# Ending each stage of a three-block transformer token block by token block, and beginning three feed-forward networks token-major

## The chip, the cores and the metric

The kernel runs on one core of a Trainium2 chip (trn2). The time is device microseconds (us) of one execution. TensorE is called PE below, VectorE DVE, ScalarE ACT, GpSimd POOL, and SyncE SP, whose queue issues the loads of the weights.

## The reference

Batch 1, 256 tokens, width 1024, float32. Three blocks run one after the other:

```
def _swiglu(t, w_gate, w_up, w_down):
    return (jax.nn.silu(t @ w_gate) * (t @ w_up)) @ w_down

# block 1, two layers
f = _swiglu(_rmsnorm(h, ffn1_pre_g[l]), ...); h = h + 0.5 * _rmsnorm(f, ffn1_post_g[l])
... attention, three branches ...
h = h + _rmsnorm(merged @ w_out[l], mix_post_g[l])
f = _swiglu(_rmsnorm(h, ffn2_pre_g[l]), ...); h = h + 0.5 * _rmsnorm(f, ffn2_post_g[l])

# block 2, two layers: mixer 0 is a spatial gating unit (SGU), mixer 1 an RWKV scan
x = layer_norm(DN_ALPHA * x + 0.5 * swiglu(x, ffn_w_in[i, 0], ffn_w_out[i, 0]), ...)
x = layer_norm(DN_ALPHA * x + mix, ...)
x = layer_norm(DN_ALPHA * x + 0.5 * swiglu(x, ffn_w_in[i, 1], ffn_w_out[i, 1]), ...)
```

Each feed-forward network (FFN) of blocks 1 and 2 has a hidden width of 2816, there are eight of them. Block 3 is not touched by the change.

## The kernel before

**Tokens.** The 256 tokens are two token blocks of 128 (b = 0, 1; `NB` = 2). The residual stream `h` lies token-major (tokens on partitions). A product needs its input feature-major (`k.x`: features on partitions, 8 tiles of 128 by 256 tokens), so between two stages `h` is normed on DVE and ACT, turned by PE transposes (line 728, `pe_features`), and copied out of PSUM as a rounded part and a rest: `x_hi` on ACT, `x_lo` on DVE (line 750).

**Weights.** All weights come as 440 units of 128x2048 floats (1 MB). SP loads unit n into one of three places of `weight_ring`; `hi` (ACT, line 118) writes the rounded weights and `lo` (DVE, line 313) the rest into one of two slots, `k.w[:, n % 2]`. `hi(n)` waits for the mark of unit n-2, which is the last product that read this slot; PE waits for `lo(n)` before it uses unit n; SP waits for `lo(n-3)` before it loads unit n. Every product is three matmuls (`mm3`, line 105): hi by hi, hi by lo, lo by hi.

**An FFN.** The hidden width is cut in 11 parts of 256. `make(j)` is the gate unit and the up unit of part j (96 matmuls of 256 columns), hidden units on partitions; ACT takes the silu (line 883), DVE multiplies (line 907), ACT and DVE split the hidden values (lines 118 and 910). `use(j)` is the down unit (24 matmuls of 512 columns, 12 for each token block), which adds into four PSUM banks `acc`, two for each token block. The order is make(0), make(1), use(0), make(2), ..., make(10), use(9), use(10). Each engine has one queue, in the order in which the code is written. `act_ffn` and `dve_ffn` put one `hi` and one `lo` behind each part, and one more behind the last: it belongs to a unit of the stage that follows.

**Between the stages.** After a stage, `add(b)` reads `acc` of token block b when that block's last product has been made, so block 0 comes half a unit ahead of block 1. In block 2 (`dve_residual`, `act_residual`) DVE's order is add(0), gain(0), add(1), norm(0), gain(1), norm(1); a block's norm needs the sum of squares and square root from ACT (lines 669, 672). Then follow `pe_features`, which opens with 12 or 24 warm matmuls on constants, and `act_features`. In block 1 (`dve_add_norm`, `act_add_norm`) ACT also reads `acc` itself, once plain and once scaled (lines 606, 613), and a second norm (lines 647 to 659) stands before the turn.

**Names.** ffn1(0), ffn2(0), ffn1(1), ffn2(1) are the FFNs of block 1 (layer in brackets); `f2(0,0)`, `f2(0,2)`, `f2(1,0)`, `f2(1,2)` those of block 2; `sgu` the SGU's down product (8 units), `w_out` the attention's output product (4 units), `w_o` that of the scan (4 units). After `w_o` every engine is drained and waits for all others (`all_drained`, line 335 is its wait).

Of the kernel before, what the change touches and what calls it, by code (L numbers as in the profile page):

```python
# [12 lines left out]
P = 128  # L13
# [210 lines left out]

class Kernel:


    def __init__(self, nc, ctx, aps):
        self.nc, self.ctx, self.aps = nc, ctx, aps
        self.s = Signals(nc, ctx)  # L230
        self.plan, self.unit_marks = [], []
        self.begin()
        self.allocate()

    def begin(self):
# [44 lines left out]
def unit(k, pe, *what, a=KT):  # L280
# [15 lines left out]
def hi(k, act):  # L296
# [3 lines left out]
    if n < len(k.plan):  # L300
        act.wait_ge(*k.s.at(f"w_raw{n % RING}", n))
        if n >= 2:
            act.wait_ge(*k.s.at(*k.unit_marks[n - 2]))
        copy_act(act, k.w.hi[:, n % 2, :], k.ring[:, n % RING, :]).then_inc(*k.s.up("w_hi", n))


def lo(k, dve):
# [368 lines left out]
def dve_residual(k, dve, of, alpha, scale, done):  # L676
# [26 lines left out]
    gain(0)  # L703
    add(1)
    norm(0)
    gain(1)
    norm(1)

# [5 lines left out]
def pe_features(k, pe, of, src, taken, warm=0, at=2, made=None, midway=None):  # L714
# [39 lines left out]
def pe_to_tokens(k, pe, src, ap, start, marks=None):  # L754

    for b in range(NB):
        for c in range(2):
            for i in range(2):
                a = mm3(pe, half(acc_of(k, b), i), src[:, c, b * P:(b + 1) * P], half(ap[:, c], i), start and c == 0)
# [4 lines left out]

def pe_output(k, pe, of, units, ready):

    for n, what in enumerate(units):
# [13 lines left out]
        else:  # L781
            for b in range(NB):
                for j in range(KT):
                    a = tile(b, j)
                if n == 3:
                    a.then_inc(*k.s.up("acc", of, b))
            if n < 3:
                a.then_inc(*k.s.up("out_unit", of, n))
        unit_done(k, *(("acc", of, 1) if n == 3 else ("out_unit", of, n)))
# [41 lines left out]
def pe_ffn(k, pe, f, gate, up, down, ready, beside={}):  # L831

    def make(j):
# [8 lines left out]
        unit_done(k, "gate", f, j, 1)  # L842
        ap = unit(k, pe, *up(j))
        for c in range(2):
# [4 lines left out]
    def use(j):  # L849
        ap = unit(k, pe, *down(j), a=2)  # L850
# [5 lines left out]
        if j < FF - 1:  # L856
            pe_to_tokens(k, pe, k.hid[:, j % 2], ap, j == 0).then_inc(*k.s.up("down", f, j))
            unit_done(k, "down", f, j)
        else:
            pe_to_tokens(k, pe, k.hid[:, j % 2], ap, False, [("acc", f, b) for b in range(NB)])  # L860
            unit_done(k, "acc", f, 1)

    for j in range(FF):
        make(j)
        if j:
            use(j - 1)
        if j in beside:
            beside[j]()
    use(FF - 1)
# [6 lines left out]
def act_ffn(k, act, f, beside={}):  # L876
    def make(j):
# [6 lines left out]
        hi(k, act)  # L884
# [6 lines left out]
    for j in range(FF):  # L891
        make(j)
        if j:
# [3 lines left out]
    hi(k, act)  # L897


def dve_ffn(k, dve, f, beside={}):  # L900
    def make(j):
        lo(k, dve)
        lo(k, dve)
# [9 lines left out]
    for j in range(FF):  # L913
        make(j)
        if j:
# [3 lines left out]
    lo(k, dve)  # L919

def memory1(k, m):
# [3045 lines left out]
```

## Time and profile before

| | |
|---|---|
| Runs shown | 3055.65, 3062.40, 3061.32 us; median 3061.32 |
| Profiled execution, its own time | 3062.81 us |
| Its span in the trace | 3061.0 us |
| Mean granted TensorE clock | 0.975 of full |
| PE busy | 2906.7 us, 95% of the span |
| DVE / ACT / POOL busy | 1704.8 / 1430.4 / 165.4 us |
| Loaded from HBM | 488.32 MB, 160 GB/s |
| A weight unit's load, issue to landing | 4.8 us median |

A start in a row is counted in us from the span's start. "PEclk" is the granted clock. A busy PE is not always one that works on weights: warm matmuls and transposes count too.

### The profile page before, as it was taken

Reading aid. Unit: us, or ns where it says so; the run is one execution under the profiler, and the core shown is the slowest. Engines: PE = TensorE matmul, PEld = TensorE weight load, DVE = VectorE, ACT = ScalarE, POOL = GpSimd, SP = SyncE. Lnnn points to the kernel's source line nnn. Section 1 sums busy time; section 2 is a strip of 40 time slices with the busy share of each in tenths; the row PEclk is TensorE's granted clock in tenths of the full one; section 3 lists DMA queues with packets and bytes.
Section 4 is the critical chain, followed back from the end, with each engine's and each line's share of the span. In section 5 each row is a group of like instructions: output and inputs, shape, how many; then the busy total and the mean of one; then the engine's idle time right before and its main releaser. Section 6 shows DMA issues by size and latency. Waiting matters only on the chain.

```text
span 3061.0 us, 53742 instructions
## 1 busy us (share of the span) xinstructions
PE 2906.7 (95%) x23664; PEld 2700.3 (88%) x23664; DVE 1704.8 (56%) x1977; ACT 1430.4 (47%) x1817; POOL 165.4 (5%) x197
## 2 busy tenths in 40 slices
PE   8999898999998998999999999999987999999998
PEld 8988898999998898999989899899877889876887
DVE  5564555545554556455455654554767454575555
ACT  4455655444455655444445344444551244454444
POOL 1000100000000010001000000000002000054000
PEclk9999999999999999999999999999979999997999
DMA  6553334554553344556554445455420145551453
GB/s 248 189 181 134 138 133 159 192 187 173 192 179 125 137 152 152 191 181 223 191 204 168 153 178 191 171 189 184 151 107 3 48 177 187 179 181 43 152 185 132
DMA packets 69393, 492.87 MB, mean 161 GB/s; under 512 B 7853, under 2 KB 9421, under 8 KB 10534
## 3 DMA queue, kind: packets, MB, share of 16 engines
q1 hardware_dynamic: 64224, 465.53, 42.5%
q10 hardware_dynamic: 4938, 23.92, 2.1%
q8 instruction: 187, 3.06, 0.4%
q14 instruction: 44, 0.36, 0.0%
HBM read 488.32 MB, written 1.06 MB: 160 GB/s over the span
## 4 chain that ended last, share of the span: by engine, by line
PE 80%; DVE 8%; ACT 7%; POOL 2%; issue 2%; PEld 0%; DMA 0%; ACTq 0%; PEldq 0%; DVEq 0%; POOLq 0%; SPq 0%
PE front L105 52%; PE acc L105 28%; ACT weights_hi L118 3%; DVE weights_lo L313 2%; POOL conv_gate L3193 1%; POOL conv_out L3196 1%; DVE tmp L690 1%; DVE h L683 1%; DVE h L698 1%; PEld acc L105 0%; ACT L1111 0%; ACT tmp L1111 0%; DVE b_x_lo L522 0%; ACT b_att_w_by_query L1013 0%; DVE b_x_lo L750 0%
## 5 line engine op out<-in xcount | busy, mean ns | idle before, releaser
L313 DVE TENSOR_TENSOR weights_lo<-weight_ring,weights_hi 128x2048 fp32r<-128x2048 f32 x440 | 1010.0, 2296 | 916.8 <-ACT weights_hi L118 916.5
L105 PE MATMUL front<-b_x_hi,weights_hi 128*128 128x256 f32 x3568 | 1011.0, 283 | 15.5 <-DVE b_x_lo L750 9.9
L118 ACT ACTIVATE weights_hi<-weight_ring 128x2048 fp32r<-128x2048 f32 x440 | 839.7, 1909 | 388.7 <-PE acc L105 355.1
L105 PE MATMUL front<-b_x_hi,weights_lo 128*128 128x256 f32 x3568 | 1005.4, 282 | 0.0
L105 PE MATMUL front<-b_x_lo,weights_hi 128*128 128x256 f32 x3568 | 1004.9, 282 | 0.0
L105 PEld LDWEIGHTS front<-b_x_hi,weights_hi 128*128 128x128 f32 x3568 | 675.3, 189 | 28.9 <-issue 13.3
L105 PEld LDWEIGHTS front<-b_x_lo,weights_hi 128*128 128x128 f32 x3568 | 675.8, 189 | 3.3
L105 PEld LDWEIGHTS front<-b_x_hi,weights_lo 128*128 128x128 f32 x3568 | 674.9, 189 | 0.0
L105 PE MATMUL acc<-weights_hi,b_hidden_hi 128*128 128x512 f32 x832 | 329.6, 396 | 0.0
L105 PE MATMUL acc<-weights_hi,b_hidden_lo 128*128 128x512 f32 x832 | 328.2, 394 | 0.0
L105 PE MATMUL acc<-weights_lo,b_hidden_hi 128*128 128x512 f32 x832 | 327.3, 393 | 0.0
L118 ACT ACTIVATE b_hidden_hi<-act_gate 128x256 fp32r<-128x256 f32 x208 | 86.9, 418 | 341.4 <-DVE act_gate L907 313.4
L883 ACT ACTIVATE act_gate<-front 128x256 f32<-128x256 f32 x176 | 67.3, 384 | 277.5 <-PE front L105 277.4
L105 PEld LDWEIGHTS acc<-weights_hi,b_hidden_lo 128*128 128x128 f32 x832 | 156.5, 188 | 37.8
L105 PEld LDWEIGHTS acc<-weights_lo,b_hidden_hi 128*128 128x128 f32 x832 | 156.7, 188 | 32.7
L105 PEld LDWEIGHTS acc<-weights_hi,b_hidden_hi 128*128 128x128 f32 x832 | 156.5, 188 | 32.6 <-DVE weights_lo L313 0.4
L105 PE MATMUL front<-weights_hi,b_x_hi 128*128 128x256 f32 (+1 forms) x496 | 142.0, 286 | 9.6 <-DVE weights_lo L313 7.6
L105 PE MATMUL acc<-b_x_hi,weights_hi 128*128 128x256 f32 x416 | 124.7, 300 | 20.5 <-ACT tmp L1111 12.7
L105 PE MATMUL front<-weights_lo,b_x_hi 128*128 128x256 f32 (+1 forms) x496 | 141.3, 285 | 0.0
L105 PE MATMUL front<-weights_hi,b_x_lo 128*128 128x256 f32 (+1 forms) x496 | 141.1, 285 | 0.0
L910 DVE TENSOR_TENSOR b_hidden_lo<-act_gate,b_hidden_hi 128x256 fp32r<-128x256 f32 x176 | 75.3, 428 | 85.2 <-ACT b_hidden_hi L118 85.2
L105 PE MATMUL acc<-b_x_hi,weights_lo 128*128 128x256 f32 x416 | 121.0, 291 | 0.0
(493 smaller groups left out, 3904.1 us busy)
## 6 DMA issues: line engine op xcount, KB each, us to landing
weight_ring<-in_weights SPq DMA_DIRECT2D x440, 1024.0 KB, 4.8
xn<-in_norm_rows ACTq DMA_DIRECT2D x14, 1024.0 KB, 4.8
sgu_bias_row<-in_sgu_rows ACTq DMA_DIRECT2D x1, 2048.0 KB, 10.9
sgu_norm_rows<-in_sgu_rows ACTq DMA_DIRECT2D x1, 2048.0 KB, 9.9
bias_hankel<-bias_scratch ACTq DMA_DIRECT2D x1, 1536.0 KB, 6.5
h<-in_x SPq DMA_DIRECT2D x2, 512.0 KB, 6.6
mem_norm<-in_memory SPq DMA_DIRECT2D x1, 1024.0 KB, 14.1
sgu_w_spatial<-in_sgu_w_spatial ACTq DMA_DIRECT2D x1, 1024.0 KB, 4.7
```

The lines of the kernel that those rows point to most:

```text
L105: return pe.matmul(out, a, b, start=start, stop=stop, skip_group_check=True)
L118: return act.activation(out, in_, ACT.Copy, scale=scale)
L313: dve.tensor_tensor(k.w.lo[:, n % 2, :], k.ring[:, n % RING, :], k.w.hi[:, n % 2, :], ALU.subtract) \
L683: dve.scalar_tensor_tensor(out=h, in0=h, scalar=alpha / scale, in1=acc_of(k, b), op0=ALU.mult, op1=ALU.add, accum_out=stat(k, 0, b)).then_ ...
L690: dve.scalar_tensor_tensor(out=k.t[:, b], in0=k.h[:, b, :], scalar=stat(k, 1, b), in1=k.rows[:, 0], op0=ALU.add, op1=ALU.mult).then_inc(*k ...
L698: dve.scalar_tensor_tensor(out=half(k.h[:, b], i), in0=half(k.t[:, b], i), scalar=stat(k, 6, b), in1=half(k.rows[:, 1], i), op0=ALU.mult, ...
L883: act.activation(k.act_gate[:, c, :], k.bank[c][:, 0:S], ACT.Silu).then_inc(*k.s.up("silu", f, j, c))
L910: dve.tensor_tensor(k.hid.lo[:, j % 2, c, :], k.act_gate[:, c, :], k.hid.hi[:, j % 2, c, :], ALU.subtract) \
L3193: pool.tensor_scalar(k.conv_sg[:, 1, :], k.conv_in[:, 1, j:j + S], k.col(("conv_dw_w_3", (0, j)), 1), None, ALU.mult).then_inc(*k.s.up("po ...
L3196: pool.tensor_tensor(k.conv[:, 1, :], k.conv[:, 1, :], k.conv_sg[:, 1, :], ALU.add) \
```

## The change

1. **Last two units block by block.** In `pe_last_two` and in `pe_output` the last two units n-1 and n of a stage run as: unit n-1 for token block 0, unit n for block 0, unit n-1 for block 1, unit n for block 1. This holds for the eight FFNs, the SGU's down product, both `w_out` and `w_o`.
2. **Two more slots.** In the FFNs (of block 2 from the up unit of f2(0,0) on), the SGU's down product and `w_out` a unit takes the one of four slots that has been unused longest; `hi` waits for the unit that used that slot last. Two slots as before hold for the other stages, the attention and `w_o` among them. At two places the second oldest slot is taken (`turned_at`).
3. **hi and lo earlier.** Part 10 of an FFN (`make(10)`) has two `hi` in front of the hidden split and three `lo` in front of the multiplication, and none stands behind the FFN. The SGU's turn has one `hi` and one `lo` ahead of its first `x_hi` and `x_lo`.
4. **Norm order.** `dve_residual` runs add(0), gain(0), norm(0), add(1), gain(1), norm(1).
5. **Token-major head.** The three FFNs behind the norms r2(0,1) (after the SGU, f2(0,2)), r2(0,2) (f2(1,0)) and r2(1,1) (after `w_o`, f2(1,2)) begin with `pe_ffn_head`: turn block 0, gate(0) of block 0, half of up(0) of block 0, turn block 1, the rest of up(0), gate(0) and up(0) of block 1. Here tokens are on partitions, so the hidden values of part 0 are turned back by four more transposes. The 24 warm matmuls of these three places are gone, and the loads of norm rows (`act_load_rows`) are issued behind part 1.
6. **No barrier.** The drain and the waits for all engines behind `w_o` are gone.

```diff
 def hi(k, act):
-        if n >= 2:
-            act.wait_ge(*k.s.at(*k.unit_marks[n - 2]))
-        copy_act(act, k.w.hi[:, n % 2, :], k.ring[:, n % RING, :]).then_inc(*k.s.up("w_hi", n))
+        slot, before = k.place[n]
+        if before is not None:
+            act.wait_ge(*k.s.at(*k.unit_marks[before]))
+        copy_act(act, k.slot[slot].hi, k.ring[:, n % RING, :]).then_inc(*k.s.up("w_hi", n))
...
     add(0)
     gain(0)
+    norm(0)
     add(1)
-    norm(0)
+    if head:
+        dve_x_block(k, dve, of, 0)
     gain(1)
     norm(1)
+    if head:
+        dve_x_block(k, dve, of, 1)
...
+def pe_last_two(k, pe, of, srcs, whats, first_mark, ready):
+    aps = []
+    for b in range(NB):
+        for n in range(2):
+            if b == 0:
+                aps.append(unit(k, pe, *whats[n], a=2))
+                for m in ready[n]:
+                    pe.wait_ge(*k.s.at(*m))
+            a = pe_block_to_tokens(k, pe, srcs[n], aps[n], b)
+            if n:
+                a.then_inc(*k.s.up("acc", of, b))
+            elif b:
+                a.then_inc(*k.s.up(*first_mark))
...
+def pe_ffn_head(k, pe, f, gate, up, of, src, warm):
+    pe_warm(k, pe, warm, 0)
+    pe_turn_block(k, pe, of, src, 0)
+    g, u = unit(k, pe, *gate), unit(k, pe, *up)
+    first, rest = range(KT // 2), range(KT // 2, KT)
+    for b in range(NB):
+        outs = [empty(k, pe, HEAD_BANKS[b][n], (("silu", "glu")[n], f, 0, b))[:, 0:S] for n in range(2)]
+        pe_block_tok(k, pe, of, g, b, outs[0], range(KT)).then_inc(*k.s.up("gate", f, 0, b))
+        if b:
+            unit_done(k, "gate", f, 0, 1)
+            pe_turn_hidden(k, pe, f, 0)
+        pe_block_tok(k, pe, of, u, b, outs[1], first)
+        if b == 0:
+            pe_turn_block(k, pe, of, src, 1)
+        pe_block_tok(k, pe, of, u, b, outs[1], rest).then_inc(*k.s.up("upper", f, 0, b))
+    unit_done(k, "upper", f, 0, 1)
...
 def act_ffn: make(j)
-        hi(k, act)
+        act_units(k, act, 2 if j == FF - 1 else 1)
 def dve_ffn: make(j)
-        lo(k, dve)
-        lo(k, dve)
+        dve_units(k, dve, 3 if j == FF - 1 else 2)
...
 def act_sgu: first turn
+                act.wait_ge(*k.s.at("bias_stored"))
+                hi(k, act)
...
 def pe_rwkv_out, act_rwkv_out, dve_rwkv_out, pool_rwkv_out
-    all_drained(k, pe, "pe", "rwkv")
```

**DVE at the end of f2(0,2)** (part 10 and the norm's first addition; line 907/1100 is the multiplication, 910/1103 the hidden rest, 683/704 add(0)), before:

```order
L313 TENSOR_TENSOR weights_lo<-weight_ring,weights_hi 128x2048 [waits s_w_hi] x3
L907 TENSOR_TENSOR act_gate<-front,act_gate 128x256 [waits s_silu,s_upper]
L910 TENSOR_TENSOR b2_hidden_lo<-act_gate,b2_hidden_hi 128x256 [waits s_hid_hi]
L907 TENSOR_TENSOR act_gate<-front,act_gate 128x256 [waits s_silu,s_upper]
L910 TENSOR_TENSOR b2_hidden_lo<-act_gate,b2_hidden_hi 128x256 [waits s_hid_hi]
L313 TENSOR_TENSOR weights_lo<-weight_ring,weights_hi 128x2048 [waits s_w_hi] x2
L683 SCALAR_TENSOR_TENSOR h,norm_stats<-h,acc 128x1024 [waits s_acc,s_loaded_rows]
```

and now:

```order
L332 TENSOR_TENSOR weights_block20_lo<-weight_ring,weights_block20_hi 128x2048 [waits s_w_hi] x2
L332 TENSOR_TENSOR weights_lo<-weight_ring,weights_hi 128x2048 [waits s_w_hi] x2
L1100 TENSOR_TENSOR act_gate<-front,act_gate 128x256 [waits s_silu,s_upper]
L1103 TENSOR_TENSOR b2_hidden_lo<-act_gate,b2_hidden_hi 128x256 [waits s_hid_hi]
L1100 TENSOR_TENSOR act_gate<-front,act_gate 128x256 [waits s_silu,s_upper]
L1103 TENSOR_TENSOR b2_hidden_lo<-act_gate,b2_hidden_hi 128x256 [waits s_hid_hi]
L332 TENSOR_TENSOR weights_block20_lo<-weight_ring,weights_block20_hi 128x2048 [waits s_w_hi]
L704 SCALAR_TENSOR_TENSOR h,norm_stats<-h,acc 128x1024 [waits s_acc,s_loaded_rows]
```

One `lo` has moved from behind the hidden split to ahead of it: four stand there instead of three, and one instead of two between it and add(0).

**ACT at the end of ffn2(1)**, the last FFN of block 1, part 10 (line 883/1014 is the silu, `s_upper` the mark of part 10's up product, 602/621 the start of the norm), before:

```order
L883 ACTIVATE act_gate<-front 128x256 [waits s_hid_lo,s_gate] x2
L118 ACTIVATE weights_hi<-weight_ring 128x2048 [waits s_gate,s_w_raw0]
L118 ACTIVATE b1_hidden_hi<-act_gate 128x256 [waits s_down,s_glu] x2
L118 ACTIVATE weights_hi<-weight_ring 128x2048 [waits s_upper,s_w_raw1]
L118 ACTIVATE weights_hi<-weight_ring 128x2048 [waits s_down,s_w_raw2]
L602 ACT_TABLE_LOAD
```

and now:

```order
L1014 ACTIVATE act_gate<-front 128x256 [waits s_hid_lo,s_gate] x2
L118 ACTIVATE weights_block10_hi<-weight_ring 128x2048 [waits s_down,s_w_raw1]
L118 ACTIVATE weights_hi<-weight_ring 128x2048 [waits s_upper,s_w_raw2]
L118 ACTIVATE b1_hidden_hi<-act_gate 128x256 [waits s_down,s_glu] x2
L621 ACT_TABLE_LOAD
L625 ACTIVATE act_gate,norm_stats<-acc 128x512 [waits s_acc]
```

Only here does the second `hi` ahead of the hidden split wait for `s_upper`, the last product of part 10 itself; the hidden split that the last down product needs stands behind it.

**DVE between the SGU and f2(0,2)** (683/704 add, 690/711 gain, 698/719 norm, 750/1045 `x_lo`), before:

```order
L313 TENSOR_TENSOR weights_lo<-weight_ring,weights_hi 128x2048 [waits s_w_hi] x2
L683 SCALAR_TENSOR_TENSOR h,norm_stats<-h,acc 128x1024 [waits s_acc,s_loaded_rows]
...
L690 SCALAR_TENSOR_TENSOR tmp<-h,norm_stats,xn 128x1024 [waits s_neg_mean]
L683 SCALAR_TENSOR_TENSOR h,norm_stats<-h,acc 128x1024 [waits s_acc]
...
L698 SCALAR_TENSOR_TENSOR h<-tmp,norm_stats,xn 128x512 [waits s_rstd]
...
L750 TENSOR_TENSOR b2_x_lo<-front,b2_x_hi 128x512 [waits s_x_hi] x2
```

and now:

```order
L704 SCALAR_TENSOR_TENSOR h,norm_stats<-h,acc 128x1024 [waits s_acc,s_loaded_rows]
...
L719 SCALAR_TENSOR_TENSOR h<-tmp,norm_stats,xn 128x512 [waits s_rstd]
L719 SCALAR_TENSOR_TENSOR h<-tmp,norm_stats,xn 128x512
L704 SCALAR_TENSOR_TENSOR h,norm_stats<-h,acc 128x1024 [waits s_acc]
...
L1045 TENSOR_TENSOR b2_x_lo<-front,b2_x_hi 128x4x128 [waits s_x_hi,s_neg_mean]
L1045 TENSOR_TENSOR b2_x_lo<-front,b2_x_hi 128x4x128 [waits s_x_hi]
L711 SCALAR_TENSOR_TENSOR tmp<-h,norm_stats,xn 128x1024
```

Block 0's norm now stands ahead of add(1), and block 0's two `x_lo` between add(1) and gain(1).

## Rows read from the trace of the kernel before

**Rows 1.** The page: span and busy times of the engines.

```profile
span 3061.0 us, 53742 instructions
PE 2906.7 (95%) x23664; PEld 2700.3 (88%) x23664; DVE 1704.8 (56%) x1977; ACT 1430.4 (47%) x1817; POOL 165.4 (5%) x197
```

**Rows 2.** PE's work on constants alone (warm, turns): window, length, busy (count), clock, DMA.

```profile
508.60:518.00 9.40, 7.25 (x63) 1.00 0.24 98
703.90:713.57 9.67, 7.35 (x64) 1.00 0.26 105
1400.00:1406.46 6.46, 5.12 (x40) 1.00 0.90 330
1595.00:1603.70 8.70, 5.41 (x22) 0.73 0.62 262
1759.50:1767.91 8.41, 5.77 (x40) 0.91 0.29 117
1955.60:1964.06 8.46, 5.31 (x40) 1.00 0.30 120
2152.40:2164.72 12.32, 6.22 (x40) 0.76 0.22 86
2454.20:2463.90 9.70, 5.54 (x40) 1.00 0.22 95
2650.80:2659.96 9.16, 6.22 (x40) 0.85 0.26 107
```

**Rows 3.** Chain that ended last, from f2(0,2)'s down(9) to f2(1,0): start, us, what.

```profile
1944.47 5.59 PE acc L105 x24
...
1950.14 1.93 ACT weights_hi L118
...
1954.30 1.23 DVE h L683 x2
...
1964.06 24.53 PE front L105 x192
```

**Rows 4.** Timeline of PE, the turn of block 1 in that stretch.

```profile
1962.11 0.66 PE L728 MATMUL front<-cons,h 128*128 128x128 f32 x4 [1.40 <-DVE h L698]
```

**Rows 5.** Timeline of DVE, part 10 of f2(0,2).

```profile
1941.03 2.29 DVE L313 TENSOR_TENSOR weights_lo<-weight_ring,weights_hi 128x2048 fp32r<-128x2048 f32 x1 [3.61 <-ACT weights_hi L118]
1943.24 0.42 DVE L907 TENSOR_TENSOR act_gate<-front,act_gate 128x256 f32<-128x256 f32 x1
...
1945.41 0.42 DVE L910 TENSOR_TENSOR b_hidden_lo<-act_gate,b_hidden_hi 128x256 fp32r<-128x256 f32 x1 [0.48 <-ACT b_hidden_hi L118]
```

**Rows 6.** Timeline of DVE: block 1's norm after f2(0,0), f2(1,0), f2(1,2).

```profile
1600.70 1.41 DVE L698 SCALAR_TENSOR_TENSOR h<-tmp,norm_stats,xn 128x512 f32<-128x512 f32 x2
2158.43 1.41 DVE L698 SCALAR_TENSOR_TENSOR h<-tmp,norm_stats,xn 128x512 f32<-128x512 f32 x2
2656.78 1.42 DVE L698 SCALAR_TENSOR_TENSOR h<-tmp,norm_stats,xn 128x512 f32<-128x512 f32 x2
```

**Rows 7.** Timeline of ACT, block 1's second square sum after w_out(0).

```profile
513.10 1.06 ACT L647 ACTIVATE act_gate<-h 128x1024 f32<-128x1024 f32 x1 [1.23 <-DVE h L636]
```

**Rows 8.** Timeline of ACT after ffn2(1): last DMA issue, first `x_hi`.

```profile
1404.54 0.32 ACTq L1714 DMA_DIRECT2D bias_table<-in_bias_table  x1
1404.90 1.08 ACT L118 ACTIVATE b_x_hi<-front 128x512 fp32r<-128x512 f32 x2 [2.45 <-PE front L728]
```

**Rows 9.** Timeline of PE, the first product after ffn1(0).

```profile
211.35 0.38 PE L105 MATMUL front<-b_x_hi,weights_hi 128*128 128x256 f32 x1 [1.35 <-DVE weights_lo L313]
```

**Rows 10.** Timeline of DVE in `w_o`: `lo` of its third unit.

```profile
2444.70 2.29 DVE L313 TENSOR_TENSOR weights_lo<-weight_ring,weights_hi 128x2048 fp32r<-128x2048 f32 x1 [3.99 <-ACT weights_hi L118]
```

**Rows 11.** Timeline of DVE, the SGU's first turn.

```profile
1706.79 0.69 DVE L1882 TENSOR_TENSOR b_x_lo<-front,b_x_hi 128x512 fp32r<-128x512 f32 x1 [0.64 <-ACT b_x_hi L118]
```

**Rows 12.** PE in make(0) of f2(0,2), f2(1,0), f2(1,2): same columns.

```profile
1767.91:1779.30 11.39, 11.39 (x89) 0.92 0.52 184
1964.06:1975.50 11.44, 11.44 (x84) 0.85 0.48 185
2463.90:2475.30 11.40, 11.40 (x96) 1.00 0.55 185
```

More of the change, by code:

```diff
@@ L237, in begin @@
         self.emptied = [()] * 8
+        self.slots, self.slot_used, self.turned = PAIR_OF_SLOTS, {}, False
         self.s.count = {}
@@ L244, in pair, with more_slots @@
         return Pair(self.sb(ctx, f"{name}_hi", shape, F32R), self.sb(ctx, f"{name}_lo", shape, F32R))
+    def more_slots(self, ctx, of, n=2, first=0):
+        w = self.pair(ctx, f"weights_{of}{first}", [P, n, UNIT])
+        for i in range(n):
+            self.slot[of, first + i] = w[:, i, :]
     def con(self, name):
@@ L756, in pe_to_tokens @@
     for b in range(NB):
-        for c in range(2):
-            for i in range(2):
-                a = mm3(pe, half(acc_of(k, b), i), src[:, c, b * P:(b + 1) * P], half(ap[:, c], i), start and c == 0)
+        a = pe_block_to_tokens(k, pe, src, ap, b, start)
         if marks:
@@ L828, with pe_ffn @@
 FF = DFF // 256
-def pe_ffn(k, pe, f, gate, up, down, ready, beside={}):
+def pe_ffn(k, pe, f, gate, up, down, ready, beside={}, head=None, slots=None, turned_at=None):
     def make(j):
@@ L842, in make @@
         unit_done(k, "gate", f, j, 1)
+        if head and j == 1:
+            pe_turn_hidden(k, pe, f, 1)
+        k.turned = turned_at == ("up", j)
         ap = unit(k, pe, *up(j))
+        k.slots = slots or k.slots
         for c in range(2):
@@ L849, in use @@
     def use(j):
+        k.turned = turned_at == ("down", j)
         ap = unit(k, pe, *down(j), a=2)
@@ L855, in use @@
             pe.wait_ge(*k.s.at("hid_lo", f, j, c))
[L856 to L863, printed above, removed]
+        pe_to_tokens(k, pe, k.hid[:, j % 2], ap, j == 0).then_inc(*k.s.up("down", f, j))
+        unit_done(k, "down", f, j)
+    if head:
+        pe_ffn_head(k, pe, f, gate(0), up(0), *head)
+        k.slots = FFN2_SLOTS
+    for j in range(1 if head else 0, FF):
         make(j)
-        if j:
+        if 0 < j < FF - 1:
             use(j - 1)
@@ L889, in make @@
             copy_act(act, k.hid.hi[:, j % 2, c, :], k.act_gate[:, c, :]).then_inc(*k.s.up("hid_hi", f, j, c))
-    for j in range(FF):
+    if head:
+        act_hidden_head(k, act, f, head)
+    else:
+        act_units(k, act, first)
+    for j in range(1 if head else 0, FF):
         make(j)
-        if j:
+        if 0 < j < FF - 1:
             hi(k, act)
@@ L911, in make @@
                 .then_inc(*k.s.up("hid_lo", f, j, c))
-    for j in range(FF):
+    if head:
+        dve_hidden_head(k, dve, f)
+    else:
+        dve_units(k, dve, first)
+    for j in range(1 if head else 0, FF):
         make(j)
-        if j:
+        if 0 < j < FF - 1:
             lo(k, dve)
@@ L1506, in act_layer @@
     act_load_rows(k, act, ("ffn2", l))
-    act_ffn(k, act, ("ffn2", l))
+    act_ffn(k, act, ("ffn2", l), first=0, two=l == 0)
     if l == L1 - 1:
@@ L1575, in dve_layer @@
     dve_features(k, dve, ("pre2", l))
-    dve_ffn(k, dve, ("ffn2", l))
+    dve_ffn(k, dve, ("ffn2", l), first=0, two=l == 0)
     if l == L1 - 1:
```

254 lines of the change are left out of this document (186 added, 68 removed).

## The prediction

> **What bounds the kernel now.** I read the page first. PE is busy for 2906.7 of 3061.0 us [rows 1], so the kernel is made of PE's products, and what can still be won lies between stages. Of "busy" a part is no product: in the windows between the last weight product of a stage and the first of the next, PE works on constants alone, 5 to 7 us of warm matmuls and turns in each 6.5 to 12.3 us [rows 2]. The nine windows named there sum to 82.3 us (9.4 to 9.67 in block 1's norms with a second norm, of which w_out(1) is one more like w_out(0)); I began each just after the product's end, so the gaps are about 0.15 us longer. Each ffn1 has a gap of 1.35 us only [rows 9]. The rest is dense: 24 down products take 5.59 us, 192 make products 24.53 us here [rows 3].
>
> Then the chain in one gap. down(9) of f2(0,2) runs from 1944.47 for 5.59 us, so down(10) runs from 1950.06 to 1955.65. The next `hi` waits for down(9) and starts at 1950.14, `lo` follows, and add(0) begins at 1954.30, though down(10)'s half for block 0 ended at 1950.06 + 2.80 = 1952.86. The first weight product comes at 1964.06 [rows 3]. Inside lie two adds, gains and norms in series, one more `x_hi`, `x_lo`, and turns, of which four start 0.66 us before the next four at most [rows 4].
>
> **The change, part by part.** E is the end of the stage's last product.
>
> *Block by block.* Block 0's `acc` is complete 5.6 us before E instead of 2.8 us. With `lo` gone from in front of add(0), block 0's whole norm can be over at E, and what is left behind E is block 1's: add 1.23 [rows 3], gain, ACT's square and root, norm. PE's own work is not changed by it, the same 24 + 24 products.
>
> *Ends without a head.* After f2(1,0) and f2(1,2) block 1's norm began at 2158.43 and 2656.78 [rows 6], both 6.0 us after their windows begin [rows 2], so E+6.15. From E on I count add 1.23, square on ACT 1.35 with the read of its sum (1.06 for the same 1024 columns in [rows 7]; I take 0.3 more), root and reciprocal 0.5, hand-overs 0.25: 3.35 us. Saved 2.8 each. After f2(0,0) it was 1600.70, 5.7 us after its window begins, so E+5.85: saved 2.5. Bounds: nothing, if ACT or the row loads set it; 5.6 us, the two halves.
>
> *Block 1's four ends.* There ACT makes the sums of both token blocks itself, and a second square starts at 513.10 [rows 7]; ACT has no free time between 508.6 and there. What is saved is that block 0 is through ahead of E: 1.0 us at each `w_out` and 1.2 at ffn2(0). After ffn2(1) the first `x_hi` stands behind six DMA issues of which the last is at 1404.54 [rows 8]; these don't move, so 0.6. In the two ffn1 the wait of 1.35 us for `lo` [rows 9] goes, since that `lo` is now made ahead: −1.35 each. Bounds: 0 and 2.8 each.
>
> *Three heads.* The new gap: add(1) 1.23, block 0's `x_lo` 0.69 (as many elements as in [rows 11]), and 0.45 for two hand-overs and the small instructions behind the addition, so 2.4 us after E. The 16 turns of rows 2 were in the gap; now 8 are in it but before E+2.4, 8 stand in the flow of products, and 4 more turn the hidden part. I price a turn at 0.11 us: a 256-column product in the row of 192 is 24.53/192 = 0.128, at a low clock partly; the other end is 0.66/4 = 0.165 [rows 3, 4]. So 12 x 0.11 = 1.35, at most 2.0. Per head, gap before minus 2.4 minus 1.35: after the SGU 8.6 − 3.75 = 4.8; after f2(0,2) 8.6 − 3.75 = 4.9; after `w_o` 9.9 − 3.75 − 0.4 = 5.7, the 0.4 because there `lo` of the third next unit stands ahead of add(0). Block 1 inside the head: DVE after add(1) (E+1.5) makes block 0's two `x_lo` (2.9), gain(1) (1.28 taken, near add's length; 4.2) and norm(1) 1.41 [rows 6] (5.7); turned by E+6.6, then two `x_hi` and `x_lo` in turns, done at E+8.4. PE's cover is block 0's gate and up, half of make's 11.4 [rows 12], and turns: 6.4 us, so gate(0) of block 1 starts at E+8.9. Half a microsecond is left. If it fails, its lateness is paid three times.
>
> *Clock.* In make(0) PE took 11.4 us in three rows with granted clocks of 0.92, 0.85 and 1.00 [rows 12]. A share 1−c at half speed costs (1−c) x 11.4: 0.9, 1.7, 0. The gaps before were 8.4 to 9.7 us with 40 matmuls on constants in them [rows 2]; now it is 2.4 us with 8. I book half of the loss as given back: 0.5 after the SGU and 0.8 after f2(0,2). Bounds: nothing, and all of it at every gap.
> Against it: the change drops 24 warm matmuls at each of the three heads. make(0) after `w_o`, with 24 of them ahead, is at 1.00, and the one after f2(0,2), with the same 24, at 0.85 [rows 12], so they did not always hold the clock. If all three heads opened as the worst of these rows, 3 x 1.7 = 5.1 us would be spent where rows 12 spend 2.6 and I have 1.3 left: 3.8 us more than my sum. The Trainium skill ("TensorE: Matmul & The Clock Gate", Part 1 and "HAM oscillation") has the clock go down to 1.2 GHz when PE stands idle for long enough and come back after sustained activity, and advises to warm up; the 0.85 row agrees that a gap filled with warm matmuls can still be followed by a slow stretch.
>
> *Stall before down(10)'s block 0.* This is new. It now begins 2.80 us after down(9) does, not 5.59. Four `lo` stand ahead of the multiplication instead of three. In f2(0,2) the third `lo` starts at 1941.03, the multiplication at 1943.24, and the hidden rest is over at 1945.83 [rows 5]. A `lo` more is 2.21 (1943.24 − 1941.03): 1948.04. PE wants it at 1944.47 + 2.80 = 1947.27. Stall 0.8 us; its `hi` (1.93, [rows 3]) runs in ACT's free time if its slot is free. Taken 0.85 in seven FFNs. Bounds: 0 and the case below.
>
> *ffn2(1).* Here the second `hi` ahead of the hidden split waits for the last product of part 10. It starts when down(9) starts, D: `hi` 1.93, `lo` 2.21, then the 2.59 us from the multiplication to the rest's end [rows 5], hand-overs 0.15: D+6.9, against D+2.8. Stall 4.1 us.
>
> *`w_o`.* With two slots the `hi` of its third unit waits for unit 1, and its `lo` starts at 2444.70 and ends at 2446.99 [rows 10]. The product of unit 3 was wanted only at the third unit's end before; now `lo` of unit 3, whose `hi` waits for unit 1, is wanted after half of unit 2 (2.83 us after its start at 2442.7): 2446.99 − 2445.5 = 1.5 us.
>
> *SGU.* An extra `lo` stands ahead of the first `x_lo`, at 1706.79 [rows 11], and its `hi` ahead of `x_hi`: 1.7 us of stall, since DVE is free only for 0.6 us before it. *Barrier:* the drain itself is inside the `w_o` gap, counted. *Slots, row loads moved behind part 1:* nothing; SP's loads wait for `lo` as before, and the norm rows have a whole FFN to arrive.
>
> **Sum.** Ends: −2.5 −2.8 −2.8 −1.0 −1.0 −1.2 −0.6 −1.35 −1.35 = −14.6. Heads −15.4, clock −1.3. Stalls: 7 x 0.85 = +5.95, ffn2(1) +4.1, `w_o` +1.5, SGU +1.7 = +13.2. Total −18.1. The span would be 3061.0 − 18.1 = 3042.9 and the profiled execution, 1.8 us above its span, 3044.7. It was 1.5 us above the median of the runs (3061.32), so the median would be 3043.
>
> **Rivals.**
> *Smaller gain.* Block 1 is late in the heads by 2 us each (cover of 0.5 us only, and turns at 0.165), or all heads open at the clock of the 0.85 row (+3.8). 3 x 2 and 2 for the turns make 8: about 3051; the clock alone makes 3047, and is a third of this case's chance. For it: DVE carries block 0's `x_lo`, gain(1), norm(1), block 1's `x_lo`, a multiplication and two `lo` in 9 us. Against: each of these has a row and they fit. That the change does nothing at a gap is the same case at its end: if block 1's norm is as late after E as before, the ends' 8.1 us go as well, 3059.
> *Larger gain.* The short gaps keep the clock up. Rows 2 have 0.73, 0.76, 0.85 in three of nine. All of the loss of rows 12 back is 1.3 more, no stall before down(10) in the seven FFNs 6.0, and 0.5 at each of the other gaps' first parts 3: near 3034. Against: DVE's `lo` has its 2.21 us in any case.
> *Slower.* The wait before down(10)'s block 0 is as long in every FFN as at ffn2(1). The mechanism: a `hi` ahead of the hidden split, waiting for a late product. Savings before stalls are 14.6 + 15.4 + 1.3 = 31 us; with the 3.2 of SGU and `w_o`, eight ends of 3.5 us bring it to zero, at 4.1 us each it is 3066. Against: only at ffn2(1) does the order show `s_upper` there.
>
> **How the numbers follow.** Main case (14 to 22 us won) 0.62, smaller gain 0.20, larger 0.11, none or slower 0.07. 0.2% is 6.1 us and about what a measurement of this kernel tells from no change. The range reaches 9 us to both sides, to the middle of the two neighbours: 3034 to 3052. Faster by over 0.2% 0.93, within 0.2% 0.04, slower 0.03.
>
> **What would show it.** In the changed profile: nine gaps; first weight product 2.4 us after the last at three of them; a wait of PE on the hidden rest in the middle of down(9)/down(10), 0.8 us in seven FFNs and 4 us at ffn2(1); in the heads no wait for block 1's `x_lo`; clock of make(0) near 1.00 behind the heads' gaps. I am wrong if PE waits over 1 us inside the heads, if the stalls at the ends exceed 2 us, or if the granted clock in the heads is below 0.85.

## The result and the profile after

The changed kernel takes 3042.08 us (median of 4 runs, 3040.09 to 3048.01), the kernel before 3060.88 us beside it. The ratio is 0.9943 with a 95% interval of 0.9927 to 0.9959, so the change is worth 12 to 22 us. The profiled execution was the longest of the four, 3048.01 us with a span of 3046.2 us. The page of the changed kernel:

```profile
span 3046.2 us, 53615 instructions
PE 2894.2 (95%) x23604; PEld 2696.4 (89%) x23604; DVE 1702.8 (56%) x1977; ACT 1421.1 (47%) x1817; POOL 170.2 (6%) x197
```

PE's busy time fell by 12.5 us although the products are the same. Inside the nine gaps below, its work on constants fell from 54.2 to 36.4 us; part of that came back as turns inside the heads, and the clock moved other stretches both ways. The same view as [rows 2], PE's work on constants alone between the last product of a stage and the first of the next (window, length, busy and count, clock, DMA share, GB/s):

```profile
511.70:520.46 8.76, 7.32 (x64) 1.00 0.00 0
708.00:716.82 8.82, 7.39 (x64) 1.00 0.00 0
1413.20:1419.09 5.89, 4.69 (x40) 1.00 0.50 170
1607.70:1613.75 6.05, 3.85 (x22) 1.00 0.00 0
1770.80:1773.50 2.70, 1.21 (x8) 1.00 0.16 67
1963.40:1965.74 2.34, 0.88 (x8) 1.00 0.00 0
2155.40:2164.80 9.40, 5.13 (x40) 1.00 0.03 9
2454.80:2457.04 2.24, 0.79 (x8) 1.00 0.12 48
2646.70:2652.92 6.22, 5.12 (x40) 1.00 0.01 3
```

Row by row against [rows 2]: the nine gaps were 82.3 us and are 52.4 us. The tenth, behind w_out(1), went from 9.5 to 8.8 us, and the waits of 1.35 us of [rows 9] behind the two ffn1 are gone. What each gave, beside what the sum had for it (the heads' turns, which were booked apart, left out):

| gap behind | before | after | saved | predicted |
|---|---|---|---|---|
| w_out(0) | 9.40 | 8.76 | 0.6 | 1.0 |
| ffn2(0) | 9.67 | 8.82 | 0.9 | 1.2 |
| ffn2(1) | 6.46 | 5.89 | 0.6 | 0.6 |
| f2(0,0) | 8.70 | 6.05 | 2.7 | 2.5 |
| SGU (head) | 8.41 | 2.70 | 5.7 | 6.2 |
| f2(0,2) (head) | 8.46 | 2.34 | 6.1 | 6.2 |
| f2(1,0) | 12.32 | 9.40 | 2.9 | 2.8 |
| w_o (head) | 9.70 | 2.24 | 7.5 | 7.1 |
| f2(1,2) | 9.16 | 6.22 | 2.9 | 2.8 |

What was paid stands in PE's timeline of the changed kernel: ffn2(1)'s down(10), the SGU's first down product, down(10) of f2(0,2), and unit 3 of w_o. The bracket is PE's idle time ahead and what ended it:

```profile
1402.29 0.77 PE L105 MATMUL acc<-weights_block_hi,b_hidden_hi 128*128 128x512 f32 x1 [4.15 <-DVE b_hidden_lo L1103]
...
1719.42 0.47 PE L105 MATMUL acc<-weights_hi,b_x_hi 128*128 128x512 f32 x1 [1.73 <-DVE b_x_lo L2096]
...
1954.85 0.47 PE L105 MATMUL acc<-weights_hi,b_hidden_hi 128*128 128x512 f32 x1 [0.89 <-DVE b_hidden_lo L1103]
...
2445.91 0.39 PE L105 MATMUL acc<-weights_hi,rwkv_out_x_hi 128*128 128x256 f32 x1 [1.55 <-DVE weights_lo L332]
```

All seven ordinary FFN ends have the wait of the third row, 0.83 to 1.01 us. All PE work from the start of each head for 12.8 us, and in ffn2(1) behind its wait:

```profile
1773.50:1786.30 12.80, 12.80 (x108) 1.00 0.18 60
1965.74:1978.54 12.80, 12.80 (x108) 1.00 0.16 55
2457.04:2469.84 12.80, 12.80 (x108) 1.00 0.17 55
1402.29:1413.10 10.81, 10.81 (x36) 0.76 0.15 64
```

Each of the first three windows holds the head's 96 products, 10 of its 12 turns and the first two products of part 1, at full clock (a granted clock of 1.00) and with no wait inside; the last two turns stand in part 1. The 36 products behind ffn2(1)'s wait take 10.8 us; at the 5.59 us for 24 of [rows 3] they would take 8.4. PE had idled for 4.15 us before them, and the granted clock is 0.76.

### The profile page after: what moved, and what is told of

The parts are those of the page before. It is cut to its first block, busy times and chain, and to the rows that moved or that the text cites. A ratio compares the mean times of both kernels' runs of the same rounds, so it can differ in the third digit from the quotient of the medians.

```text
span 3046.2 us, 53615 instructions
## 1 busy us (share of the span) xinstructions
PE 2894.2 (95%) x23604; PEld 2696.4 (89%) x23604; DVE 1702.8 (56%) x1977; ACT 1421.1 (47%) x1817; POOL 170.2 (6%) x197
## 4 chain that ended last, share of the span: by engine, by line
PE 80%; ACT 7%; DVE 7%; POOL 2%; issue 2%; DMA 0%; ACTq 0%; POOLq 0%; DVEq 0%; SPq 0%
PE front L105 51%; PE acc L105 29%; DVE weights_lo L332 2%; ACT weights_hi L118 2%; POOL conv_gate L3404 1%; POOL conv_out L3407 1%; ACT L1309 1%; DVE weights_block_lo L332 1%; ACT b_att_w_by_query L1211 1%; ACT tmp L1309 0%; DVE h L704 0%; ACT weights_block_hi L118 0%; ACT L1211 0%; DMA weight_ring<-in_weights 0%; ACT act_gate L690 0%
## 5 line engine op out<-in xcount | busy, mean ns | idle before, releaser
L332 DVE TENSOR_TENSOR weights_lo<-weight_ring,weights_hi 128x2048 fp32r<-128x2048 f32 x298 | 682.0, 2294 | 546.9 <-ACT weights_hi L118 546.7
L105 PE MATMUL front<-b_x_hi,weights_hi 128*128 128x256 f32 x2096 | 596.0, 284 | 9.5 <-DVE b_x_lo L777 6.8
L105 PE MATMUL front<-b_x_hi,weights_lo 128*128 128x256 f32 x2096 | 593.2, 283 | 0.0
L105 PE MATMUL front<-b_x_lo,weights_hi 128*128 128x256 f32 x2096 | 592.8, 283 | 0.0
L332 DVE TENSOR_TENSOR weights_block_lo<-weight_ring,weights_block_hi 128x2048 fp32r<-128x2048 f32 x137 | 315.5, 2313 | 303.7 <-ACT weights_block_hi L118 303.5
L105 PEld LDWEIGHTS front<-b_x_lo,weights_hi 128*128 128x128 f32 x2096 | 398.6, 190 | 1.8
L105 PEld LDWEIGHTS front<-b_x_hi,weights_lo 128*128 128x128 f32 x2096 | 398.6, 190 | 0.0
L105 PE MATMUL front<-b_x_hi,weights_block_hi 128*128 128x256 f32 x1376 | 389.6, 283 | 2.5 <-DVE b_x_lo L777 2.5
L105 PE MATMUL front<-b_x_hi,weights_block_lo 128*128 128x256 f32 x1376 | 389.2, 283 | 0.0
L105 PE MATMUL front<-b_x_lo,weights_block_hi 128*128 128x256 f32 x1376 | 389.1, 283 | 0.0
## 6 DMA issues: line engine op xcount, KB each, us to landing
sgu_bias_row<-in_sgu_rows ACTq DMA_DIRECT2D x1, 2048.0 KB, 10.7
```

Of the source, the lines that this page charges most:

```text
L105: return pe.matmul(out, a, b, start=start, stop=stop, skip_group_check=True)
L332: dve.tensor_tensor(w.lo, k.ring[:, n % RING, :], w.hi, ALU.subtract) \
```

## The experiments

**e1: the extra `lo` behind the hidden split.** Theory: the waits before down(10) come from the `hi` and `lo` that the change moved ahead of the hidden split. Rivals: the hidden values would be as late without that (B), or the time comes back in the gaps (C).

```diff
 def act_ffn: make(j)
-        act_units(k, act, 2 if j == FF - 1 else 1)
+        hi(k, act)
         for c in range(2): ... hid_hi
+        if j == FF - 1:
+            hi(k, act)
 def dve_ffn: make(j)
-        dve_units(k, dve, 3 if j == FF - 1 else 2)
+        dve_units(k, dve, 2)
         for c in range(2): ... hid_lo
+        if j == FF - 1:
+            lo(k, dve)
```

> The changed kernel, but in part 10 of all eight FFNs one hi and one lo go back behind the hidden split (as before the change they stood there), everything else as changed. Theory A, the wait of PE before down(10)'s first block comes from this one lo (and, at ffn2(1), from its hi that waits for part 10's up product): the seven waits of 0.85 to 0.95 us and the one of 4.15 us at ffn2(1) all go, and down(10) of ffn2(1) runs at full clock again (10.8 us back to 8.4); 12 us less than the changed kernel, about 3030. Rival B, the hidden values are simply not there earlier: the waits stay, 3042. Rival C, the lo now delays add(0) and the gaps grow by what the waits shrink: also 3042, but with gaps longer by 1 to 2 us each.

3030.89 us, ratio 0.9907 (0.9886 to 0.9929), so by the ratios 11 us below the changed kernel (3 to 19). All eight waits are gone. DVE's timeline of the changed kernel at the end of f2(0,2), then that of this one:

```profile
1947.73 4.49 DVE L332 TENSOR_TENSOR weights_lo<-weight_ring,weights_hi 128x2048 fp32r<-128x2048 f32 x2 [6.34 <-ACT weights_hi L118]
1952.14 0.42 DVE L1100 TENSOR_TENSOR act_gate<-front,act_gate 128x256 f32<-128x256 f32 x1
...
1954.28 0.43 DVE L1103 TENSOR_TENSOR b_hidden_lo<-act_gate,b_hidden_hi 128x256 fp32r<-128x256 f32 x1 [0.48 <-ACT b_hidden_hi L118]
```

```profile
1935.29 2.29 DVE L332 TENSOR_TENSOR weights_lo<-weight_ring,weights_hi 128x2048 fp32r<-128x2048 f32 x1 [6.34 <-ACT weights_hi L118]
1937.50 0.42 DVE L1102 TENSOR_TENSOR act_gate<-front,act_gate 128x256 f32<-128x256 f32 x1
...
1939.73 0.42 DVE L1105 TENSOR_TENSOR b_hidden_lo<-act_gate,b_hidden_hi 128x256 fp32r<-128x256 f32 x1 [0.48 <-ACT b_hidden_hi L118]
1941.54 2.29 DVE L332 TENSOR_TENSOR weights_lo<-weight_ring,weights_hi 128x2048 fp32r<-128x2048 f32 x1 [1.39 <-ACT weights_hi L118]
1943.75 2.29 DVE L332 TENSOR_TENSOR weights_block_lo<-weight_ring,weights_block_hi 128x2048 fp32r<-128x2048 f32 x1
```

With two `lo` (4.49 us in one row) ahead, the hidden rest ends at 1954.71, and PE starts at 1954.85; with one, it ends 4.9 us after the `lo` began instead of 7.0. In this kernel's chain of waits down(9) and down(10) are one unbroken piece, where the changed kernel has 0.14 us of issue and 36 products behind it:

```profile
1938.79 11.07 PE acc L105 x48
```

Rival C holds at one place only: where two `lo` now stand ahead of add(0) (behind f2(0,2)) the gap is 0.6 us longer. The other gaps are unchanged to 0.1 us. The cause of the waits is shown.

**e2: the heads taken out.** Theory A: of what the three head gaps saved, the earlier `acc` and the norm order carry a part, the heads the rest.

```diff
 def pe_next2(...):
-    pe_ffn(k, pe, f, *units, None, head=(norm, k.h, 0), turned_at=turned_at)
+    pe_features(k, pe, norm, k.h, in_parts(norm), warm=12)
+    pe_ffn(k, pe, f, *units, split_mark(norm), turned_at=turned_at, slots=FFN2_SLOTS)
```

(ACT and DVE likewise: act_features, dve_features, and no x_lo within the norm.)

> The changed kernel with its three token-major heads taken out: pe_features with 24 warm matmuls and feature-major part 0 as before, loads of norm rows before the FFN as before, norm order without the x_lo of block 0 in between; last two units by block, four slots and no barrier stay. Theory A (heads and earlier ends each bring a part): the three gaps are near the 6.2 us of the gap after f2(0,0) instead of 2.4 to 2.9, and part 0 is 1.5 us shorter for its 12 turns; 3 x 2.3 = 7 us more, about 3049. Rival B (the heads bring nearly all at these places): gaps back at 8.6 to 9.9, 15 us more, 3057. Rival C (the clock falls again behind the longer gaps, 0.9 to 1.7 us in make(0)): 2 to 4 us on top of A, 3052.

3053.15 us, ratio 0.9987 (0.9977 to 0.9998). PE's work on constants in the three gaps:

```profile
1765.90:1772.37 6.47, 4.92 (x40) 1.00 0.06 23
1961.00:1967.08 6.08, 4.90 (x40) 1.00 0.00 0
2452.70:2458.71 6.01, 4.84 (x40) 1.00 0.11 48
```

They are 11.3 us longer than the changed kernel's; parts 0 and 1 have 12 turns less, about 1.3 us in each FFN (ten of them make the difference between 12.6 and 11.5 us for the 96 products). By the places that is 7.5 us, as A had it, and the span of this trace is 7.8 us over that of the changed kernel's second trace (e6). The medians differ by 11 us and the two ratios allow 8 to 19, so by the medians the heads are worth more than the places show; what makes the difference is not known. So of the 5.7, 6.1 and 7.5 us saved in the three gaps, 3.8 us each is the token-major head (2.5 net of turns), and 1.9, 2.4 and 3.7 us is what the stage ends get without it, the barrier's removal included in the last.

This run also brings the warm matmuls back, as many as before the change. They don't lengthen these gaps: PE waits for block 1's norm behind them (0.55 us in the second gap). And here they may have done something for the clock. Rival C isn't seen: all three make(0) run at 1.00 behind gaps of 6.0 to 6.5 us, with 95 instructions in 11.40 us each. The first of them:

```profile
1772.37:1783.77 11.40, 11.40 (x95) 1.00 0.52 184
```

**e3: the last two units one after the other again.**

```diff
 def pe_last_two(...):
-    for b in range(NB):
-        for n in range(2):
-            if b == 0:
+    for n in range(2):
+        ...
+        for b in range(NB):
```

(In pe_output likewise.)

> The changed kernel, but the last two units of every stage run unit by unit again (both token blocks of one, then both of the other), with the slots, the earlier hi and lo, the heads, the norm order and no barrier as changed. Theory A: block 0's sums are complete 2.8 instead of 5.6 us before the end, so each of the ten gaps grows by 1.5 to 2.5 us (about 20 in all), while the waits before down(10) go (0.9 in seven FFNs, 1.3 to 3.7 of the one at ffn2(1), 1.5 in w_o; about 10): 10 us more than the changed kernel, 3052. Rival B, the earlier hi and lo and the norm order alone carry the gain, since before them lo stood ahead of add(0): gaps grow by under 0.5 us and with the waits gone the time is 3035.

3041.70 us, ratio 0.9951 (0.9934 to 0.9968): the same as the changed kernel within the intervals. PE's work on constants in the three head gaps:

```profile
1757.30:1761.56 4.26, 1.27 (x8) 1.00 0.19 81
1951.80:1956.05 4.25, 1.27 (x8) 1.00 0.06 25
2442.70:2446.73 4.03, 1.27 (x8) 1.00 0.59 246
```

The six gaps of block 2 grew by 1.6 to 1.9 us, 10.9 in all; block 1's four gaps stayed at 8.8 and 5.9 us. Behind two of the three longer head gaps the 96 products of make(0) took 14.1 us instead of 12.6, which is 3 us more. All seven ordinary waits went and the one at ffn2(1) fell from 4.15 to 1.35; the one in w_o went too. Neither A nor B: in the changed kernel the block-by-block order wins 11 us in the gaps and 3 in the clock behind them, and costs about as much in the waits that it creates.

**e4: the SGU's extra `lo` behind its first `x_lo`.**

```diff
 def act_sgu: first turn
-                hi(k, act)
             copy_act(act, sgu_parts(k, 2 * n).hi, turned_pair(k, n))...
+            if n == 0:
+                hi(k, act)
```

(And `lo` in dve_sgu.)

> The changed kernel, but the extra hi and lo of the SGU's first turn stand behind its first x_hi and x_lo. Theory A (the extra lo ahead of x_lo costs 1.5 us): the pause before the first SGU down product falls from 6.2 to about 4.7 us as before the change, the rest of the down product unchanged. Rival B: another lo is late next (that of unit 1), and PE waits 1 to 2 us one unit later instead.

3047.78 us in its one run, which alone says nothing on 1.5 us. In PE's timeline the first down product now waits 0.26 us, as before the change, instead of 1.73:

```profile
1717.02 0.47 PE L105 MATMUL acc<-weights_hi,b_x_hi 128*128 128x512 f32 x1 [0.26 <-DVE b_x_lo L2095]
```

The SGU's down product takes 51.4 us from there, the same as in the changed kernel, so nothing is late next.

**e5: e1 and e4 together.**

> Both edits together: part 10's extra hi and lo behind the hidden split in all eight FFNs, and the SGU's extra hi and lo behind its first x_hi and x_lo. Theory A (the two waits are independent): 12 us plus 1.5 us less than the changed kernel that runs beside it, ratio to the kernel before near 0.990, about 3029. Rival B (one of them is given back in a later gap): 12 us less at most, and the SGU's down product ends no earlier.

3025.28 us, ratio 0.9878 (0.9848 to 0.9908): faster than either kernel. Theory A's direction holds, 18 us less than the changed kernel beside it (3043.32) where 13.5 were expected. By the places it is 16: 7.2 at ffn2(1) (against the changed kernel's trace of e6), 1.15 in each of seven FFNs, 1.5 in the SGU, minus 0.6 behind f2(0,2). All PE work of ffn2(1), first here, then in the changed kernel:

```profile
1214.93:1401.10 186.17, 186.17 (x1320) 1.00 0.50 187
```

```profile
1220.09:1413.08 192.99, 188.84 (x1320) 0.98 0.49 180
```

The kernel before took 186.15 us for it: the wait and the clock behind it are all of the 6.8 us.

**e6: the changed kernel again.**

> The changed kernel once more, unaltered, beside the others on this chip: how far its time and its stretches outside the change move between executions. If the differences outside the change (start 1.8 us, attention 1.3 and 4.5 us slower, block 3 7.8 us faster in the first trace) belong to the change, they come again; if they are the granted clock of one execution, they come out otherwise. Median 3042, ratio 0.994.

3043.32 us, ratio 0.9941 (0.9919 to 0.9962). The gaps and waits come out to 0.05 us as in the first trace. Attention of layer 1 took 278.1 us here, 282.5 in the first trace, 278.0 before the change: the clock of one execution. Block 3 took 391.5 us and didn't come back to 401, so that needed a second and third trace of the kernel before (below).

**e7: the barrier back.**

```diff
 def pe_rwkv_out, act_rwkv_out, dve_rwkv_out, pool_rwkv_out
+    all_drained(k, ..., "rwkv")
```

> The changed kernel with the drain and the wait of all engines behind w_o put back on PE, ACT, DVE and POOL. Theory A: add(0) of block 0 can't start before PE's last product has ended, so block 0's whole norm (add 1.2, gain and ACT's square and root 2.0, norm 1.4) comes behind the end again, and the gap grows from 2.4 to about 7 us. Rival B (the barrier cost nothing by itself, its wait lay under the last unit): the gap stays under 3 us.

3052.52 us in its one run. The gap is 6.93 us instead of 2.24. DVE's timeline shows add(0) held until PE's end, and both additions in series behind it:

```profile
2454.82 1.22 DVE L704 SCALAR_TENSOR_TENSOR h<-h,acc 128x1024 f32<-128x1024 f32 x1 [4.54 <-PEq L354]
...
2459.39 1.22 DVE L704 SCALAR_TENSOR_TENSOR h<-h,acc 128x1024 f32<-128x1024 f32 x1
```

On top of the rest of the change, removing the barrier is worth 4.7 us in the gap. Behind the longer gap the granted clock was 0.88 in the head, whose 96 products took 14.1 us instead of 12.7. What removing it alone would bring wasn't run.

**e8: warm matmuls in the heads, twice as many as before the change.**

```diff
-    pe_ffn(k, pe, f, *units, None, head=(norm, k.h, 0), turned_at=turned_at)
+    pe_ffn(k, pe, f, *units, None, head=(norm, k.h, 24), turned_at=turned_at)
```

> The changed kernel with 24 warm matmuls put ahead of the turn of block 0 in each of the three heads. Theory A (the clock of make(0) is at 1.00 behind a pause of 2.4 us anyway): nothing to win, the turn of block 0 comes 2.6 us later and each of the three gaps grows by about 2.2 us, 6.6 us in all; make(0) takes 12.8 us as without. Rival B (the pause costs clock that the profile's row hides): make(0) gets shorter than 12.8 us.

3062.97 us in its one run. A warm matmul is two records in the trace (48 and the 8 turns here), so these 24 are twice what the kernel before had in such a gap, and hold PE for 5.4 us, not the 2.7 us that 24 records take in e2. The gaps grew by 4.7, 5.0 and 5.1 us; the first of them:

```profile
1768.30:1775.65 7.35, 6.21 (x56) 1.00 0.05 18
```

The heads' products run as without them, at 1.00 in all three. Theory A: behind a gap of 2.4 us there is nothing for them to win, and in the head they stand ahead of the turn that everything waits for. As many as before the change (24 records) weren't tried here.

**e9 and e10: what the orders are worth once the waits are gone.** Both of these start from the kernel of e5: unit by unit as in e3, and the old order of the norm.

```diff
     gain(0)
-    norm(0)
     add(1)
+    norm(0)
```

> The kernel of e5_late_and_sgu with the last two units of every stage unit by unit again. Here no wait before down(10) is left that the old order could save (1.6 us in w_o alone), so it shows what the order is worth by itself. Theory A: six gaps of block 2 grow by 1.6 to 1.9 us as in e3, block 1's four don't, minus 1.6 in w_o, plus up to 3 us of clock behind the longer gaps: 9 to 12 us more than e5, ratio to the kernel before near 0.991. Rival B (the order brings nothing once lo is out of the way): same as e5.

> The kernel of e5_late_and_sgu with the old order of the norm in block 2: add(0), gain(0), add(1), norm(0), gain(1), norm(1). Theory A: with block 0's sums 5.6 us before the end, norm(0) is through before add(1) can start; the old order makes it wait for PE's end, the three head gaps grow by 2 us each and the three other ends by 1 us each: 9 us more than e5. Rival B (DVE is free enough either way): gaps as in e5, same time.

Unit by unit: 3035.98 us, ratio 0.9922 (0.9907 to 0.9937), 10.7 us more than e5. Old norm order: 3039.73 us, ratio 0.9932 (0.9909 to 0.9956), 14.5 us more. Both ran beside another set of runs than e5; by the ratios it is 13.5 us (3 to 24) and 16.5 us (5 to 28). Unit by unit, the six gaps of block 2 grew by 10.3 us and w_o's wait went. With the old norm order the three head gaps grew by 2.0, 2.2 and 2.3 us and the other three by 1.1 each, 9.8 in all, as expected; the clock behind them, which the expectation left out, comes on top. PE in the heads' make(0), unit by unit first, then the old norm order; the gaps ahead were 4.3, 4.2, 4.1 us and 4.7, 5.1, 4.7 us:

```profile
1757.55:1770.35 12.80, 12.80 (x97) 0.88 0.07 15
1951.84:1964.64 12.80, 12.80 (x96) 0.87 0.07 14
2442.29:2455.09 12.80, 12.80 (x108) 1.00 0.17 58
```

```profile
1757.82:1770.62 12.80, 12.80 (x87) 0.78 0.00 1
1954.29:1967.09 12.80, 12.80 (x94) 0.85 0.05 9
2450.37:2463.17 12.80, 12.80 (x85) 0.76 0.01 1
```

In the same 12.80 us only 85 to 97 of 108 instructions were through in five of six cases. At 0.12 us for each that is missing it is 2.7 us unit by unit and 6.9 us with the old norm order. Theory A holds for both: neither order is idle once the waits are gone.

**e11 and e12: the kernel before, twice more.**

> The kernel before the change once more, unaltered, for a second trace of it. Block 3, which the change doesn't touch, took 401.0 us from its first product to the end in the first trace and 389 to 397 us in all traces with the change. Theory A (granted clock of one execution): it comes out under 397 us here. Rival B (the change shortens block 3, through the clock that it meets after the last FFN or the time of its loads): it is 400 us or more again.

> The same kernel a third time, since one more trace can't tell a spread from a shift. Expected as for the run beside it: under 397 us in block 3 if it is the clock of single executions, 400 us or more if it belongs to the kernel.

All PE work of block 3 in these two traces:

```profile
2656.95:3048.60 391.65, 364.23 (x2804) 0.97 0.40 145
```

```profile
2663.89:3058.00 394.11, 367.23 (x2804) 0.96 0.40 144
```

So 401 us was the clock of one execution. In it 43 products, shortly behind a wait of 0.88 us for POOL, ran at a granted clock of 0.52 in 12.9 us; the same stretch in the changed kernel (44 products, behind a wait of 0.54 us) took 7.6 us at 1.00. Block 3 has no part in the gain.

## Why the prediction held, point by point

**The total: right, and the last few us by luck.** 3043 was forecast and 3042 measured. The sum of the working was −18.1 us at places, and by the places it is less than that. Between the second traces of both kernels (e11 and e6) all stretches that the change touches differ by 12.8 us, and the ratios of two independent jobs say 12 to 22 and 12 to 25. The last 5 us between places and medians go with the mean clock of the runs, which is on record for each: beside e6 it was 0.975 in the median for the kernel before and 0.980 for the changed one. At the same mean clock of 0.980, four runs of the kernel before have spans of 3049.8 to 3054.6 us and four of the changed one 3037.9 to 3043.4, about 13 us apart. Why the changed kernel is granted more clock isn't shown beyond the places below. So the working was about 5 us too high at the places, and clock that it hadn't counted made up for it.

**Ends and heads: right.** Block 2's gaps came within 0.5 us of the working, with the norm of block 1 as what is left behind E. A part of the small difference is a reading: the working took the gaps to be 0.15 us longer than the windows of [rows 2], but behind the SGU the last product ended at 1759.50 and behind f2(0,2) at 1955.61, so there was nothing to add.

Block 1's were forecast at 1.0 and 1.2 and gave 0.6 to 0.9; e3 and e9 show that there the block-by-block order gives nothing at all, since the gaps stay at 8.8 us without it. The chain of the changed kernel behind w_out(0), whose last product ends at 511.65, shows why. It is block 1's own chain from the end of the last product on, and block 0 is through before it in either order:

```profile
511.69 0.70 ACT act_gate L625 x2
...
514.92 2.94 PE front L105 x24
517.86 0.44 PE front L755 x4
```

What was saved is DVE's work on block 0, which before the change stood behind the last product (line 636 from 508.93 to 510.26) and in front of block 1's. The chain also runs through 24 records of warm matmuls. The first half of block 1 is normed at about 518.0 and its turn starts at 518.57, so by this estimate they cost up to 0.6 us at each of these gaps; no run left them out.

The inside of the heads (half a microsecond of cover) held: no wait of PE between their products in any trace.

**Stall before down(10): right, slightly low.** 0.83 to 1.01 us of wait against 0.85; removing it gave 1.15 us, since PE also restarts slowly: the 36 products behind it take 8.57 us in the changed kernel's chain, where 36 of e1's unbroken 48 (11.07 us) take 8.30.

**ffn2(1): the mis-sized term.** The step reads "Stall 4.1 us". The wait was 4.15 us, and it came about as the working said: ACT's `hi` starts at 1395.42 and PE goes on 6.87 us later, for the D+6.9 of the working. But the place cost 6.8 us (192.99 against 186.15): the working stopped at the wait and left out that products behind this pause run slow, 2.4 us over 36 of them.

**`w_o` and SGU: right.** A wait of 1.55 us for 1.5 (the whole of `w_o` is 1.8 us longer, 27.1 for 25.3), and 1.5 us for 1.7.

**Clock: right in sign, too small, and badly read.** The three windows of [rows 12] were of equal length by my own choice, so "PE took 11.4 us in three rows" says nothing. What differs is the count, 89, 84 and 96 products. By the count 0.8 and 1.4 us were lost behind two of the gaps, near the 0.9 and 1.7 worked out from the clock, and both came back in full: 2.2 to 2.6 us where I booked 1.3. In the other two traces of the kernel before the three make(0) lost 2.7 us (e11) and 3.6 us (e12), shared otherwise among the heads.

The warm matmuls that the change dropped were not missed: make(0) is at 1.00 behind gaps of 2.2 to 2.7 us without any, and with twice as many (e8) it is no faster, while each gap is 5 us longer. Behind the longer gaps of e3, e9 and e10 (4.1 to 5.1 us), without any, it fell in seven of nine cases. But behind gaps of 6.0 to 6.5 us with 24 records of warm matmuls (e2) it did not fall in any of three. So it isn't the length of the gap alone: in these gaps PE stood idle for 1.5 us in all in the changed kernel and for 1.2 to 1.5 us in e2. It was 2.8 to 3.4 us in e3, e9 and e10 and 2.7 to 4.3 us in the three traces of the kernel before, and there the clock fell in 15 of 18 cases.

The Trainium skill ("TensorE: Matmul & The Clock Gate", Part 1 and "HAM oscillation") has the clock depend on how long PE stands idle. The traces agree for these gaps: the shorter idle time goes with the full clock. The 0.52 of block 3, behind a wait of only 0.88 us, isn't explained by it.

**The rivals.** The slower one needed a late `hi` ahead of every hidden split; only ffn2(1) had it, as the order of ACT said. The smaller gain through a late block 1 didn't happen. That the order of the last two units brings nothing in the end was not among my cases: what it gains in the gaps and its waits cancel in the changed kernel (e3), and only with the `lo` behind the split does it pay, 10.7 us by the medians (e9). No run takes the two further slots away or puts all `hi` and `lo` back to their old places, so what these parts of the change bring by themselves stays open.

## What to carry to other kernels

When a producer is reordered so that a consumer can begin earlier, look at what the new order asks for earlier itself: here down(10) was wanted 2.8 us sooner, and the `lo` that had been moved out of the norm's way landed in its way. Place work made ahead behind the last thing that the current stage needs, not ahead of it. Read clock losses by counting instructions in windows of equal length. And take several traces before a difference in an untouched stage is put down to a change.

## What the runs showed of the hardware

- Granted clock behind a gap between stages: gaps of 2.2 to 3.0 us with 8 turns in them left make(0) at 1.00 in all nine heads of the changed kernel's two traces and e5's; gaps of 4.1 to 5.1 us, also with 8 turns, left it at 0.76 to 0.88 in five of six (e9, e10). Gaps of 6.0 to 6.5 us with 24 records of warm matmuls and 16 turns left it at 1.00 in three of three (e2). A wait of 4.15 us in the middle of ffn2(1) left 0.76 in one trace and 0.72 in the other.
- A single execution met a stretch of block 3 at 0.52 where another had 1.00 (block 3 took 401.0 us against 391.5 to 394.1). Traces of the same kernel had spans of 3061.0, 3048.6 and 3058.0 us.
